# Routed experts of an encoder layer: the second weights asked for by ScalarE, the first weights by SyncE alone

## The reference, cut to what matters

```python
def run_block(args):
    t_idx, g, e = args
    xb = x_pad[t_idx]
    hb = jax.nn.silu(xb @ w_e_gate[e]) * (xb @ w_e_up[e])
    return (hb @ w_e_down[e]).astype(f32) * g[:, None]
...
routed = jnp.zeros((T + 1, D), f32).at[buf_tok].add(yb.reshape(P, D))[:T]
```

## Time and profile before

| | us |
|---|---|
| median of 3 runs (1741.64 to 1747.07) | 1744.38 |
| the profiled execution, its own time | 1746.64 |
| its span, first to last instruction | 1744.80 |
| PE busy in the span | 1664.4 |
| ACT busy in the span | 327.6 |
| routed rounds, from the first product to the last | 1113 to 1658 |

### The profile page before, as it was taken

One profiled execution on the slowest core, in us unless ns is written; L12 is line 12 of the kernel. 1 busy time (PEld: TensorE's weight loads), 2 busy tenths in 40 slices (PEclk: granted clock), 3 DMA queues, 4 the chain that ended last, 5 costly groups with the idle time before them and its releaser, 6 DMA issues.

```text
span 1744.8 us, 23342 instructions
## 1 busy us (share of the span) xinstructions
PE 1664.4 (95%) x9535; PEld 825.8 (47%) x9535; DVE 653.1 (37%) x1038; ACT 327.6 (19%) x518; POOL 135.2 (8%) x139
## 2 busy tenths in 40 slices
PE   7999999999999999999999999999999899899967
PEld 3444455666666555555554554433333333333323
DVE  5010127888888856441113776300000000000008
ACT  1111112222222221111000220122212212112112
POOL 0000000000000000000001113311111111111010
PEclk9999999999999999999999999999999999999989
DMA  6115101111101001201136008599999999999858
GB/s 226 48 49 166 52 13 48 37 36 36 32 30 35 25 13 48 73 24 43 54 113 230 25 25 356 220 421 423 423 425 421 423 421 421 412 402 420 344 202 363
DMA packets 104846, 330.56 MB, mean 189 GB/s; under 512 B 8224, under 2 KB 64704, under 8 KB 86592
## 3 DMA queue, kind: packets, MB, share of 16 engines
q1 hardware_dynamic: 91664, 291.69, 42.5%
q0 software_dynamic: 13104, 37.76, 5.5%
HBM read 306.36 MB, written 33.03 MB: 195 GB/s over the span
## 4 chain that ended last, share of the span: by engine, by line
PE 75%; DMA 15%; DVE 8%; issue 1%; ACT 1%; SPq 0%; DVEq 0%; POOL 0%; POOLq 0%; ACTq 0%
PE pA L1134 13%; PE pg L711 11%; PE pg L739 11%; PE pB L1160 5%; PE pB L948 5%; DMA rEF<-w_e_gate_up 4%; DMA rCD<-w_e_gate_up 4%; PE pg L752 2%; PE pA L997 2%; PE pB L997 2%; PE pA L940 2%; DMA rA<-y_dram 2%; DMA rB<-w_e_gate_up 2%; DMA ew<-w_e_gate_up 2%; PE pA L905 1%; PE pg L905 1%
## 5 line engine op out<-in xcount | busy, mean ns | idle before, releaser
L739 PE MATMUL pg<-rA,hw 128*128 128x384 f32 x768 | 264.5, 493 | 0.7 <-ACT aTr L1270 0.7
L1134 PE MATMUL pA<-rCD,aTr 128*32 128x512 f32 (+2 forms) x720 | 217.1, 610 | 8.1 <-DMA rB<-w_e_gate_up 4.4
L1939 DVE TENSOR_TENSOR rows<-rows,pA 128x256 f32<-128x256 f32 x44 | 18.5, 421 | 528.7 <-ACT rows L1412 528.7
L711 PE MATMUL pg<-rEF,rA 128*128 128x512 f32 x448 | 196.2, 600 | 5.1 <-ACT rCD L1249 3.1
L739 PEld LDWEIGHTS pg<-rA,hw 128*128 128x128 f32 x768 | 140.3, 190 | 86.5 <-ACT aTr L1270 0.9
L711 PEld LDWEIGHTS pg<-rEF,rA 128*128 128x128 f32 x448 | 85.8, 193 | 112.1 <-issue 109.7
L1134 PE MATMUL pA<-rB,aTr 128*32 128x512 f32 (+1 forms) x448 | 116.3, 602 | 6.5 <-DMA rEF<-w_e_gate_up 3.7
L1134 PE MATMUL pA<-ew,aTr 128*32 128x512 f32 (+1 forms) x272 | 112.0, 624 | 8.0 <-DMA rEF<-w_e_gate_up 5.3
L1134 PE MATMUL pA<-rA,aTr 128*32 128x512 f32 (+1 forms) x336 | 114.8, 605 | 0.0
L1134 PE MATMUL pA<-rEF,aTr 128*32 128x512 f32 (+1 forms) x384 | 112.0, 616 | 0.1
L1160 PE MATMUL pB<-rCD,rows 128*32 128x512 f32 (+2 forms) x360 | 108.8, 595 | 0.0
(11 more groups left out here) (382 smaller groups left out, 2349.1 us busy)
## 6 DMA issues: line engine op xcount, KB each, us to landing
rCD<-w_e_gate_up SPq DMA_DIRECT2D x21, 2048.0 KB, 30.1
rA<-w_e_gate_up SPq DMA_DIRECT2D x11, 2048.0 KB, 30.6
rB<-w_e_gate_up SPq DMA_DIRECT2D x11, 2048.0 KB, 28.4
ew<-w_e_gate_up SPq DMA_DIRECT2D x11, 2048.0 KB, 30.3
rEF<-w_e_gate_up SPq DMA_DIRECT2D x11, 2048.0 KB, 29.4
rCD<-w_e_down SPq DMA_DIRECT2D x21, 1024.0 KB, 31.6
hw<-w_in SPq DMA_DIRECT2D x36, 512.0 KB, 4.1
rA<-w_e_down SPq DMA_DIRECT2D x11, 1024.0 KB
```

Source lines behind the costliest of these rows:

```text
L711: last = mm(big_bank(fill), x1T[:, c, i * P:(i + 1) * P], strip[n % 2][:, c, :], start=(c == 0), stop=(c == KC - 1))
L739: last = mm(pg[:, n * 512:n * 512 + HALF], hw3[m][:, c, :], x1T[:, c, n * HALF:(n + 1) * HALF], start=(c == 0), stop=(c == KC - 1))
L1134: last = mm(gu[n][o:o + w, :], xT[n][:, c, o:o + w], at(gate_up_home(j % NB)[0], gate_up_home(j % NB)[1] + c * F, [[2 * D, 2], [1, F]]), s ...
```

## The change

The loads of second weights in the rounds move from SP to ACT. On SP the second inner loop goes. On ACT a new function `next_down(t)` stands behind `weighted(t)`, the copy of the result of round t: for each expert whose last round is t it reads the number of the expert six turns on and asks for that expert's second weights. It has no wait written for `y_filled`, because `weighted(t)` ahead of it on ACT has waited for that. ACT waits once for the row of experts (`blki_ready`) ahead of the rounds. The loads of the first six experts, and those of the short loop behind the rounds, stay on SP.

```diff
@@ on SP
                     if last_round(j) == t:
                         sp.wait_ge(gu_filled, t + 1)
                         load_gate_up(expert_in_turn(j + NB), j % NB)
-                for j in range(E - NB):
-                    if last_round(j) == t - 1:
-                        sp.wait_ge(y_filled, t)
-                        load_down(expert_in_turn(j + NB), j % NB)
@@ on ACT
+            def next_down(t):
+
+                for j in range(E - NB):
+                    if last_round(j) == t:
+                        n = j % NB
+                        e = sc.value_load(blki[0:1, j + NB:j + NB + 1], min_val=0, max_val=E - 1)
+                        sc.dma_start(down_rows[n], d["w_e_down"][bass.ds(e, 1), :, :].rearrange("e p n -> (e p) n")).then_inc(s_wd[n], 16)
+
+            sc.wait_ge(blki_ready, 1)
             gathered(0)
             gathered(1)
             for t in range(NR):
                 silu(t)
                 if t >= 1:
                     weighted(t - 1)
+                    next_down(t - 1)
                 hidden_turned(t)
```

## The result

| kernel | median of its runs, us | lowest to highest | ratio to before, 95% interval |
|---|---|---|---|
| before | 1745.72 | 1741.64 to 1751.09 | 1 |
| changed | 1768.99 | 1764.14 to 1770.66 | 1.0131 [1.0111, 1.0152] |

The change makes the kernel 23.3 us slower. The direction of the forecast and the turn-taking behind it hold. The size doesn't (1757 us was forecast, and the range ended at 1766), and one step of the mechanism fails. The profiled execution took 1767.70 us (span 1765.9). In the lines of the changed kernel the numbers of PE and ACT are 4 lower: the transposition is L1117, the first products L1130, the second products L1156, the copy of a result L1422; ACT's new issue is L1430.

A forecast was written before the change was run, and what follows sets the result against it. The prediction took the routed experts to be bound by bytes moved over DMA. Issuing and clock were priced 0; 12.9 us for weights loaded too early, added to the median 1744.38 us, gave 1757 us, range 1742 to 1766 us.

The forecast's parts named there:

- SP's issuing: Routed experts: taking 58 second-weight loads off SP gets nothing sooner, since SP waits for first products anyway; price 0.
- ACT's issuing: Routed experts: reading and issuing after the result copy hides in 5.76 us free on ACT, against 2.2 us; price 0.
- the bound of 2.9 us: Time per issue on ACT at which the free time before the next silu no longer hides the issuing.
- The turns: DMA engines serve queues row by row; a third loaded queue cuts POOL's queue from 24 to about 15 rows per us.
- Ask to landing: Routed experts: time from asking for first weights to their landing falls from 30.6 to 15.4 us.
- the stock: Weights lying ready too early, 5.4 MB at 417 GB/s, a single loss of 12.9 us shown at the stage's end.
- DMA stays busy in both kernels: Routed experts: bytes moved by any time stay the same, rounds settle at 13.0 us, so the loss is not per round.
- The clock: Routed experts: slower PE rounds behind waits (8.77 us for 7.00) add nothing, as bytes bind such rounds anyway; price 0.
- A: Rival: nothing moves; weight queues share one turn or gathers land soon enough; price 0, 1744 us; chance 0.22.
- B: Rival: first weights, alone in their queue, overtake second weights and shorten PE's waits; 4 to 7 us faster, 1739 us; chance 0.10.
- C: Rival: issuing on ACT isn't hidden and makes rounds with two issues late; 1753 to 1780 us; chance 0.04.

The follow-up runs named there:

- e3: Kernel before, all its loads still on SP, with ACT also reading 58 registers and issuing 58 unused 128 B DMAs behind the result copy: 1745.72 us, ratio 1.0010.
- e4: Changed kernel, with each load of first weights asked for as two DMAs of 8 KB rows instead of one of 16 KB rows: 1755.18 us, ratio 1.0055.
- e10: Changed kernel with all weight rows halved, first weights in 8 KB rows and second weights in 4 KB rows: 1758.05 us, ratio 1.0066.
- e7: Kernel before, with ACT asking for the second weights of every other expert and SP for the rest: 1747.69 us, ratio 1.0018.

## Why the prediction was wrong in size

**SP's issuing, price 0: right.** In the changed kernel SP still waits for PE's first products before it asks, 41 times between 1100 and 1700 us, so no first load goes out sooner for its shorter list.

**ACT's issuing, price 0: right,** by e3. One issue takes 0.34 us (ACT asks 0.97 us after its copy starts, at 1290.20 and 1291.17 in its time line), and a second follows the first by about 1.0 us (1525.05 and 1526.08); the bound of 2.9 us was never near.

**The turns: right.** One row from each queue, 14.6 rows per us for q0 where 14.9 were forecast, gathers after 20.7 us, waits at the transposition for gathers, and those for first weights gone. (A slip beside it: 5.5 us of longer service don't eat a spare of 6.3 in one round; the 2.2 us a round do the rest.) The prediction's rule was drawn from two queues; the runs show it for three, and e4 and e10 move the shares with the rows' sizes. The Trainium skill ("DMA: Bandwidth & Descriptors", "Queues, rings and completion order") says that a DMA engine goes round the queues that hold work; the 178, 186 and 176 rows agree. It has an engine take a whole packet of some 9 to 17 descriptors before it turns to the next queue; in this trace single rows alternate.

**Ask to landing, 15.4 us: right.** 12.6 to 15.0 us measured. That it should be the time between an expert's two asks, no run tests. From it came the stock, 12.9 us; the end of the stage shows 14.3. This term was 1.4 us too small.

**"DMA stays busy in both kernels": wrong, and this is the step that failed.** The prediction went on that a weight queue runs dry at times and so gives q0 its turns back, until "the mean round settles at 13.0 us again. So the loss is not per round, but one stock". That looked at the three queues as if there were always another to take the free turn. But a weight load is asked for by PE's progress, through buffers that come free, and the buffers are few. While PE stood before a late gather, both weight queues finished all that they had, and the gather's last rows don't fill 16 engines: 94 GB/s at 1550 us. Bytes not moved then are moved later. It happened five times, around 1285, 1380, 1471, 1551 and 1620 us, and made the engines 12 us more idle than before. The prediction had the last weights land a little earlier; they land 9.4 us later, and of the sum given for that above, the 12 us of idle time are the largest part. The very number that sized the stock said so: if all that is asked for lands within 15 us, and a wait can stretch the time between two asks to 17.7 us, nothing is left in the queues. With a time from ask to landing of 30 us there was always work ahead; as I read it, shortening it took away the cover of the DMA engines as well as the order.

How the idle time divides among the five places in what it costs isn't settled, nor was it tried whether one more weight buffer would remove them.

**The clock, price 0: not borne out.** Behind a wait PE runs slower for a while. In the chain of the changed kernel (start, us), after a gather the transposition takes 1.98 us where it takes 0.89, and the products 8.74 for 7.00:

```profile
1583.19 26.13 DMA hw<-x_dram,rows
...
1609.37 1.98 PE pg L1117 x8
1611.35 8.74 PE pA L1130 x64
...
1624.04 0.89 PE pg L1117 x8
1624.93 7.02 PE pA L1130 x32
```

From 1609.4 to 1611.3 us the granted clock is 0.50, the lower of its two levels (1.2 GHz); PE had waited 4.7 us for the gather before. The first products of the whole stage are busy for 320.9 us before and 321.6 after, so for them the clock is no term of the difference: the kernel before had such rounds behind its own waits. The transpositions, which now come right behind the waits, are another matter (the stage; busy us of PE in them, before and after):

```profile
1113.00:1658.00 545.00, 45.82 (x349) 0.98 0.98 407
```

```profile
1111.00:1680.00 569.00, 52.22 (x346) 0.97 0.95 390
```

That is 6.4 us more. The prediction took nothing because such rounds would be bound by bytes anyway; here PE waits for gathers and the DMA engines run dry, so they aren't always. The 6.4 us lie within the 23.7 and not beside them: by PE's own account the stage's 24 us are 14 of more idle time and 10 of more busy time. How much of the 6.4 us reaches the end, and how much of it is the clock, no run separates.

**The rivals.** A fell: the queues don't share one turn, and the gathers weren't in time. The Trainium skill's sentence for it (the same page, "Issuing engines are not separate DMA queues": asking from several engines saves only issue time) has the saving right, nothing here, but not the cost: a further loaded queue changes who is served, by 23.3 us in these runs. B fell with the equal turns: first weights did come sooner, by half, and PE had no use for it. C fell by e3.

## What to carry to other kernels

Where DMA queues take turns by rows, as they do here, opening another queue for large transfers takes service from a queue with small ones; before adding one, divide the rows that the smallest queue must move in a round by its new share, and compare with the round. Where bytes bind a stage, the order of one queue, the order of need, was worth keeping here (e4 and e10): two queues load something too early, and something else, that PE then waits for, too late. And a short time from ask to landing is no gain in itself: if it falls below the time between two asks, nothing is left to load in between.

## What was unexpected

A gather whose row numbers lie outside the table still sends a packet of a few bytes for each row that it doesn't move, 4608 in all, and takes 17.5 us to land among two loaded queues; it isn't a way to take a gather's turns out of an experiment.

Halving rows isn't free: with 8 KB and 4 KB rows for 16 KB and 8 KB ones the kernel before is 6.7 us slower [1.0019, 1.0052], though its gathers land after 10.8 us instead of 14.5.

Half of the change costs 2.3 us and the whole 23.3 (e7): a queue's loss of service costs little as long as it stays within the spare of its customers, 6.3 us for a gather here.
